# The modulation product in rows of 1024 columns, and low weight parts of three stages on VectorE

## The chip, the cores and the metric

The kernel runs on one core of a Trainium2 chip. The metric is the device time of one execution in microseconds. Before the change the median of 3 runs is 2245.02 us (2243.89 to 2248.35).

## The reference

Two transformer layers and a third, mixed one over 512 tokens of width 1024, all in float32. What matters here is the first layer and the vector that conditions it:

```python
c_act = silu(c)                                   # one row of 1024
mod = c_act @ ada_w[layer] + ada_b[layer]         # 1024 x 6144, for both layers
sh_m, sc_m, g_m, sh_f, sc_f, g_f = split(mod, 6)
h = rms_norm(x) * g * (1 + sc_m) + sh_m
u, v = split(gelu(h @ w_in + b_in), 2)            # gMLP, 2048 wide each
v = layer_norm(v); v = tril(w_s) v + b_s
x = x + g_m * rms_norm((u * v) @ w_out)
h = rms_norm(x) * g * (1 + sc_f) + sh_f
x = x + g_f * rms_norm((silu(h @ w_g) * (h @ w_u)) @ w_down)
k, v, dcum = shared_kv(x, c_act @ kv_ada_w + kv_ada_b, ...)
```

The modulation product is a row of 1024 times matrices of 6144, 2048 and 6144 columns, some 59 MB of weights, of which each element is used once.

## The kernel before

Five engines run their own instruction streams and meet at semaphores. A matrix product keeps float32 precision by splitting both operands in a high part (fp32r, rounded) and a low part (the rest): each weight times activation becomes three TensorE products, hi x hi, hi x lo and lo x hi. The work is a list of stages: mlp_u, mlp_v, mlp_out, gu0, down0, then k, v, q and so on. A stage has groups (i, j) of 256 output columns, a group has units of up to 4 chunks of 128 rows. mlp_u and mlp_v have 8 groups of 2 units, mlp_out 4 of 4, gu0 22 of 2, down0 4 of 6.

A unit's way: SP loads it into one of 4 slots of the tile `raw` (`load_unit`), once `w_used` says that TensorE has finished with the unit four before. ScalarE rounds it into `w_hi` (`split_hi`, L700). GpSimd subtracts, `w_lo = raw - w_hi`, in place of raw (`split_lo`, L706). TensorE waits for `w_split` and uses it (`gemm`, L1258). `lead` orders the splitting engines: the split of group g+1 stands before the epilogue of group g, that of group g+2 behind it. TensorE has two accumulators `acc`, so an epilogue has one group's time.

The activations go a similar way: VectorE writes tmp (`normed`), ScalarE rounds (`hi_chunks`), GpSimd subtracts (`lo_chunks`).

The modulation product is spread beside the stages as 56 steps of 256 columns. A step loads 1024 x 256 weights in two halves (`ada_load`, rows of 1 KB), VectorE multiplies each chunk of 128 rows by its column of c_act and adds (`ada_step`, L1625 and L1629, 8 instructions), and TensorE sums over the partitions with two products of one column (`ada_column`, L1309), which VectorE adds to the bias (`ada_finish`, L1634). Steps 0 to 7 belong to the setup and stay as they are. Steps 8 to 45 are one per group in mlp_u, mlp_v and gu0; TensorE's column products for a step stand at the end of the group and wait for `ada_ready`. Steps 46 to 55 are in down0. SP's order is written by hand: in these stages the weights of a group, then the step's two halves, each behind `ada_used`.

In gu0 the epilogue of a group is: ScalarE takes silu (L934), VectorE multiplies (L1816) and rounds to act_hi (L1818), GpSimd subtracts (act_lo, L1193). In mlp_v VectorE adds the bias (L1766), ScalarE takes gelu, and VectorE its statistics (L1771). mlp_u's epilogue is ScalarE's alone. The gains of an output stage are spread over the partitions by TensorE (`spread_gain`, L1316) from a diagonal that VectorE makes (`gain_diagonal`, L1672); for down0 TensorE does this at chunk 16 of the first group.

mlp_u, mlp_v and gu0 are hardware loops over i, mlp_out and down0 are unrolled.

Of the kernel before, what the change touches and what calls it, by code (L numbers as in the profile page):

```python
# [30 lines left out]
ds = bass.ds  # L31
# [26 lines left out]
ADA_STEPS = 56  # L58
DOWN_STEP, DOWN_FROM, DOWN_EVERY = 46, 24, 6
# [21 lines left out]
class Stage:  # L81


    def __init__(self, name, iters, kchunks, reader, token_major=False, second=None):
        self.name, self.iters, self.reader, self.token_major = name, iters, reader, token_major
# [9 lines left out]
    Stage("mlp_u", 4, DC, "act"), Stage("mlp_v", 4, DC, "dve", True), Stage("mlp_out", 2, GC, "dve", True),  # L95
    Stage("gu0", 11, DC, "dve"), Stage("down0", 2, FC, "dve", True),
# [10 lines left out]
def number_stages():  # L107

    unit = group = 0
    count = {"act": 0, "dve": 0}  # L110
    for s in STAGES:
        s.unit0, s.group0, s.read0 = unit, group, count[s.reader]
# [7 lines left out]
def build_program(nc, io):  # L120
    S = number_stages()
    ctx = ExitStack()
    with ctx:
# [51 lines left out]
        sq = place("sq", [P, 2, T])  # L175
        inv_diag = place("inv_diag", [P, NB, P])
# [19 lines left out]
        ada_raw = place("ada_raw", [P, 2, KU, COLS], at=ph + 88 * K)  # L196
# [86 lines left out]
        w_split = sem("w_split")  # L283
# [128 lines left out]
        def ada_round(step):  # L412

            return step - ADA_SETUP

        def ada_load(sp, w, c0, step):
            n = ada_round(step)
            for half in range(2):
                sp.wait_ge(ada_used, 2 * n + half + 1)
                sp.dma_start(ada_raw[:, half], w[half * 512:half * 512 + 512, ds(c0, COLS)].rearrange("(k p) n -> p k n", p=P)) \  # L420
                    .then_inc(ada_landed[half], 16)
# [298 lines left out]
        def _(sp):  # L720
# [36 lines left out]
            KV0, KV1 = 24, 32  # L757
            for i in range((KV1 - KV0) // 2):
                for j in range(2):
                    load_group(sp, "gu0", i, j)  # L760
                    ada_load(sp, kv_ada_w, COLS * (2 * i + j), KV0 + 2 * i + j)
            def layer1(i, j):
                ada_load(sp, ada_w[1], COLS * (KV0 - KV1 + 2 * i + j), KV0 + 2 * i + j)
            load_stage(sp, "gu0", layer1, skip=KV1 - KV0)
            st, step = S["down0"], DOWN_STEP
            for g in range(st.groups):
                for x, (k0, nk) in enumerate(st.units[g % 2]):
                    load_unit(sp, st, src_of["down0"], g // 2, g % 2, x)
# [371 lines left out]
        def _(pool):  # L1140
# [39 lines left out]
            lead(pool, "mlp_v", split_lo, nothing, None)  # L1180
# [5 lines left out]
            lead(pool, "mlp_out", split_lo, nothing, "gu0", unroll=True)  # L1186
# [8 lines left out]
            lead(pool, "gu0", split_lo, gu_epilogue, "down0")  # L1195
# [56 lines left out]
        def _(pe):  # L1252
# [8 lines left out]
            def gemm(name, hi, lo, ready, ready0, after=None, unroll=False, second=None, before_chunk=None):  # L1261
# [4 lines left out]
                def body(i):  # L1266
                    for j in range(2):
# [31 lines left out]
            def ada_column(step, par, setup=False):  # L1299

                n = step - ADA_PAIRS
                pe.wait_ge(ada_ready, n + 1)
                if not setup:
                    pe.wait_ge(ada_col, n + 1)
                column_sums(ada_ps[:, 2 * par:2 * par + 2], ada_acc[:, par, :]).then_inc(ada_sum, 1)

# [796 lines left out]
```

## Time and profile before

| | |
|---|---|
| device time, median of 3 | 2245.02 us |
| span of the profiled execution, first to last instruction | 2241.8 us |
| TensorE products busy | 2021.4 us (90%) |
| VectorE, ScalarE, GpSimd busy | 935.1, 766.3, 1009.6 us |
| mean granted TensorE clock | 0.957 |
| DMA, mean | 104 GB/s |

The page gives no time of its own execution beside the span; the median of the runs lies 3.2 us above it. TensorE's products are pipelined, so that its busy time overlaps itself and a stage is better read by its length, its count of products and its waits. Idle time of another engine says nothing unless TensorE waits for it. mlp_u runs from 53.0 to 152.4 us, mlp_v from 160.3 to 260.9, mlp_out from 285.5 to 380.8, gu0 from 401.4 to 684.2 and down0 from 684.7 to 823 us.

### The profile page before, as it was taken

Reading aid. Unit: us, or ns where it says so; the run is one execution under the profiler, and the core shown is the slowest. Engines: PE = TensorE matmul, PEld = TensorE weight load, DVE = VectorE, ACT = ScalarE, POOL = GpSimd, SP = SyncE. Lnnn points to the kernel's source line nnn. Section 1 sums busy time; section 2 is a strip of 40 time slices with the busy share of each in tenths; the row PEclk is TensorE's granted clock in tenths of the full one; section 3 lists DMA queues with packets and bytes.
Section 4 is the critical chain, followed back from the end, with each engine's and each line's share of the span. In section 5 each row is a group of like instructions: output and inputs, shape, how many; then the busy total and the mean of one; then the engine's idle time right before and its main releaser. Section 6 shows DMA issues by size and latency. Waiting matters only on the chain.

```text
span 2241.8 us, 32732 instructions
## 1 busy us (share of the span) xinstructions
PE 2021.4 (90%) x12052; PEld 1770.2 (79%) x12052; DVE 935.1 (42%) x1624; ACT 766.3 (34%) x1198; POOL 1009.6 (45%) x573
## 2 busy tenths in 40 slices
PE   5999897899999978999997999999799993987997
PEld 5789897777779976977886888899667883766897
DVE  6567742676654654544633100010337720125212
ACT  3422332432321233345644333322423320445323
POOL 2443373554454325455644555544423440625452
PEclk8999999899999989999998999999899997898999
DMA  7644323355553532222112333322212335211122
GB/s 261 196 155 151 121 68 103 108 164 164 173 171 122 190 109 59 84 76 88 52 49 61 99 94 94 102 85 91 73 57 66 94 94 85 84 38 38 48 95 85
DMA packets 274914, 232.47 MB, mean 104 GB/s; under 512 B 15017, under 2 KB 268753, under 8 KB 274561
## 3 DMA queue, kind: packets, MB, share of 16 engines
q1 hardware_dynamic: 274312, 230.97, 33.6%
q8 instruction: 68, 1.11, 0.2%
q10 hardware_dynamic: 504, 0.15, 0.0%
q14 instruction: 30, 0.24, 0.0%
HBM read 226.33 MB, written 4.75 MB: 103 GB/s over the span
## 4 chain that ended last, share of the span: by engine, by line
PE 73%; DVE 14%; DMA 3%; ACT 3%; issue 3%; DVEq 2%; SPq 1%; POOL 1%; ACTq 1%
PE acc L1258 62%; DVE ada_acc L1629 7%; PE ms L602 2%; PE acc L577 2%; DMA raw<-in_w_in 2%; DVE ada_acc L1625 1%; DVE x_tok L1707 1%; PE aux L591 1%; PE aux L1258 1%; SPq L356 1%; DMA x_tok<-in_x 1%; PE ada_ps L1309 1%; DMA ada_raw<-in_ada_w 1%; PE aux L1440 1%; DVEq L1709 1%
## 5 line engine op out<-in xcount | busy, mean ns | idle before, releaser
L706 POOL TENSOR_TENSOR w_lo<-raw,w_hi 128x1024 fp32r<-128x1024 f32 (+1 forms) x300 | 720.6, 2416 | 805.3 <-ACT w_hi L700 804.8
L1258 PE MATMUL acc<-hh,w_hi 128*128 128x512 f32 x1344 | 540.4, 402 | 45.4 <-ACT ogate L994 38.3
L1258 PE MATMUL acc<-hl,w_hi 128*128 128x512 f32 x1344 | 532.1, 396 | 0.0
L1258 PE MATMUL acc<-hh,w_lo 128*128 128x512 f32 x1344 | 532.0, 396 | 0.0
L700 ACT ACTIVATE w_hi<-raw 128x1024 fp32r<-128x1024 f32 (+1 forms) x300 | 308.6, 1040 | 505.0 <-DMA raw<-in_ffn_w_down 202.3
L1258 PEld LDWEIGHTS acc<-hh,w_hi 128*128 128x128 f32 x1344 | 258.2, 192 | 107.9 <-ACT ogate L994 38.7
L1258 PEld LDWEIGHTS acc<-hh,w_lo 128*128 128x128 f32 x1344 | 257.6, 192 | 55.5
L1258 PEld LDWEIGHTS acc<-hl,w_hi 128*128 128x128 f32 x1344 | 257.8, 192 | 54.8 <-issue 2.0
L1629 DVE SCALAR_TENSOR_TENSOR ada_acc<-ada_raw,c_act,ada_acc 128x256 f32<-128x256 f32 x336 | 265.5, 790 | 29.4 <-DMA ada_raw<-in_ada_w 3.5
L1258 PE MATMUL acc<-w_hi,hh 128*128 128x256 f32 x704 | 201.1, 286 | 0.7 <-issue 0.7
L1258 PE MATMUL acc<-w_hi,act_hi 128*128 128x256 f32 x704 | 201.6, 286 | 0.0
L1258 PE MATMUL acc<-w_hi,act_lo 128*128 128x256 f32 x704 | 199.9, 284 | 0.0
L1258 PE MATMUL acc<-w_lo,act_hi 128*128 128x256 f32 x704 | 199.9, 284 | 0.0
L1258 PE MATMUL acc<-w_lo,hh 128*128 128x256 f32 x704 | 199.2, 283 | 0.0
L1258 PE MATMUL acc<-w_hi,hl 128*128 128x256 f32 x704 | 199.2, 283 | 0.0
L1816 DVE TENSOR_TENSOR tmp<-acc,tmp 128x512 f32<-128x512 f32 x44 | 30.4, 691 | 314.4 <-ACT tmp L934 311.2
L1193 POOL TENSOR_TENSOR act_lo<-tmp,act_hi 128x512 f32 (+1 forms) x44 | 56.9, 1293 | 187.0 <-DVE act_hi L1818 187.0
L1258 PEld LDWEIGHTS acc<-w_hi,hh 128*128 128x128 f32 x704 | 135.1, 192 | 1.9 <-issue 1.4
L1258 PEld LDWEIGHTS acc<-w_hi,act_hi 128*128 128x128 f32 x704 | 135.9, 193 | 0.5 <-issue 0.5
L1258 PEld LDWEIGHTS acc<-w_lo,act_hi 128*128 128x128 f32 x704 | 135.8, 193 | 0.5 <-issue 0.5
L1258 PEld LDWEIGHTS acc<-w_hi,act_lo 128*128 128x128 f32 x704 | 135.8, 193 | 0.0
L1258 PEld LDWEIGHTS acc<-w_lo,hh 128*128 128x128 f32 x704 | 135.1, 192 | 0.8 <-issue 0.7
(367 smaller groups left out, 3086.9 us busy)
## 6 DMA issues: line engine op xcount, KB each, us to landing
raw<-in_ffn_w_gu SPq DMA_DIRECT2D x176, 256.0 KB, 3.2
ada_raw<-in_ada_w SPq DMA_DIRECT2D x80, 512.0 KB, 3.9
raw<-in_w_in SPq DMA_DIRECT2D x52, 512.0 KB, 3.4
raw<-in_ffn_w_down SPq DMA_DIRECT2D x40, 512.0 KB, 3.4
raw<-in_a_w_in SPq DMA_DIRECT2D x32, 512.0 KB, 5.0
raw<-in_a_w_out SPq DMA_DIRECT2D x16, 512.0 KB, 3.4
ada_raw<-in_kv_ada_w SPq DMA_DIRECT2D x16, 512.0 KB, 3.3
raw<-in_kv_w SPq DMA_DIRECT2D x16, 512.0 KB, 3.5
```

Source lines behind the costliest of these rows:

```text
L356: sp.dma_start(dst, ap).then_inc(landed[s], 16)
L577: pe.matmul(bank(b)[:, 0:WIDTH[b]], a["qz"][:, e, b * P:(b + 1) * P], a["k"][:, ds(i, 1), 0:WIDTH[b]].rearrange("p a t -> p (a t)"), start ...
L591: last = pe.transpose(out[:, c:c + P], a["p"][:, e, OFF[b] + s * P:OFF[b] + (s + 1) * P], ident[:])
L602: last = pe.matmul(ms[:, b * 64:b * 64 + 64], a["pT"][:, c:c + P], a["v"][:, s, ds(h * 64, 64)], start=s == 0, stop=s == b)
L700: act.activation(w_hi[:, s, 0:nk, :], raw[:, s, 0:nk, :], ACT.Copy).then_inc(w_split_hi, 1)
L706: pool.tensor_tensor(w_lo[:, s, 0:nk, :], raw[:, s, 0:nk, :], w_hi[:, s, 0:nk, :].bitcast(F32), ALU.subtract).then_inc(w_split, 1)
L1193: pool.tensor_tensor(act_lo[:, ds(f, 1), :], tmp[:, 2 + j:3 + j, :], act_hi[:, ds(f, 1), :].bitcast(F32), ALU.subtract).then_inc(act_ready, 1)
L1258: ins = pe.matmul(out, w, x, start=first and n == 0, stop=last and n == len(pairs) - 1, skip_group_check=check)
L1309: ins = pe.matmul(dst[:, m:m + 1], src[:, m * P:(m + 1) * P], ones[:, 0:1], start=True, stop=True)
L1440: pe.matmul(aux[:, t % 2, :], head_ones[:], sq[:, t % 2, :], start=True, stop=True).then_inc(hs_ps, 1)
L1629: ins = dve.scalar_tensor_tensor(total, w[:, kk, :], c_act[:, k0 + kk:k0 + kk + 1], total, ALU.mult, ALU.add)
L1816: dve.tensor_tensor(tmp[:, 2 + j, :], sums(j)[:, 1, :], tmp[:, j, :], ALU.mult).then_inc(acc_read["dve"], 1)
```

## The change

- The modulation product behind the setup is made in 12 wide steps of 1024 columns. A chunk n is one load of 128 x 1024 (rows of 4 KB) and one VectorE instruction over 1024 columns into `ada_wide`; 8 chunks make a wide step. A slot is two chunks; there are 48 slots.
- TensorE's column products are 8 per wide step (`wide_columns`), at chunk 2 of the first group of the next four (`wide_beside`), by name in mlp_out and down0. The two at every group's end go.
- Slots 0 to 7 lie in mlp_u, 8 to 15 in mlp_v, 16 to 23 behind the first two `product_group`s of mlp_out, 24 to 45 in gu0, 46 and 47 between gu0's last epilogue and down0's gain diagonal. Down0's own steps go.
- w_lo of mlp_u, mlp_v and gu0 is made on VectorE. There `lead` puts the split of the next group before the slot and the epilogue. mlp_u's first two units stand between chunks 3 and 4 of h0, gu0's first two in `add_normed` behind x_tok. `w_split` becomes one semaphore per engine.
- The three stages' loops are unrolled on the engines that the change touches (SP, TensorE, VectorE); for gu0 GpSimd's is unrolled too.

```diff
+    Stage("mlp_u", 4, DC, "act", lo="dve"), Stage("mlp_v", 4, DC, "dve", True, lo="dve"), Stage("mlp_out", 2, GC, "dve", True),
+    Stage("gu0", 11, DC, "dve", lo="dve"), Stage("down0", 2, FC, "dve", True),
...
+        def ada_load(sp, n):
+            wide, k = 2 + n // DC, n % DC
+            w, c0 = (ada_w[0], wide) if wide < 6 else (kv_ada_w, wide - 6) if wide < 8 else (ada_w[1], wide - 8)
+            sp.wait_ge(ada_used, n + 1)
+            sp.dma_start(ada_raw[:, n % 2, :], w[k * P:(k + 1) * P, ADA_WIDE * c0:ADA_WIDE * (c0 + 1)]).then_inc(ada_landed[n % 2], 16)
+        def ada_slot_load(sp, slot):
+            ada_load(sp, 2 * slot)
+            ada_load(sp, 2 * slot + 1)
...
+                eng.wait_ge(w_split_hi, unit_no(st, i, j, x) + 1)
+                eng.tensor_tensor(w_lo[:, s, 0:nk, :], raw[:, s, 0:nk, :], w_hi[:, s, 0:nk, :].bitcast(F32),
+                                  ALU.subtract).then_inc(w_split[st.lo], 1)
...
+            ada_slot_load(sp, 0)
+            ada_slot_load(sp, 1)
+            load_stage(sp, "mlp_u", lambda i, j: ada_slot_load(sp, 2 * i + j), skip=2, unroll=True)
+            load_stage(sp, "mlp_v", lambda i, j: ada_slot_load(sp, 8 + 2 * i + j), unroll=True)
+            load_group(sp, "mlp_out", 0, 0)
+            load_group(sp, "mlp_out", 0, 1)
+            st = S["mlp_out"]
             for j in range(2):
-                ada_load(sp, ada_w[0], COLS * (8 + j), 8 + j)
-            load_stage(sp, "mlp_u", lambda i, j: ada_load(sp, ada_w[0], COLS * (8 + 2 * i + j), 8 + 2 * i + j), skip=2)
-            load_stage(sp, "mlp_v", lambda i, j: ada_load(sp, ada_w[0], COLS * (16 + 2 * i + j), 16 + 2 * i + j))
-            load_stage(sp, "mlp_out")
...
+                for x in range(len(st.units[j])):
+                    ada_slot_load(sp, 16 + len(st.units[0]) * j + x)
+                    load_unit(sp, st, src_of["mlp_out"], 1, j, x)
+            load_stage(sp, "gu0", lambda i, j: ada_slot_load(sp, 24 + 2 * i + j), unroll=True)
+            load_group(sp, "down0", 0, 0)
+            ada_slot_load(sp, 46)
+            ada_slot_load(sp, 47)
+            load_stage(sp, "down0", skip=1)
...
-            split_lo(pool, S["mlp_u"], 0, 0)
             lo_chunks("h0", DC, hh, hl)
-            lead(pool, "mlp_u", split_lo, nothing, "mlp_v")
...
-            lead(pool, "mlp_v", split_lo, nothing, None)
             split_lo(pool, S["mlp_out"], 0, 0, slice(0, 1))
             for x in range(GC // KU):
                 lo_chunks("y", KU, y_hi, y_lo, KU * x)
                 split_lo(pool, S["mlp_out"], 0, 0, slice(x + 1, x + 2))
-            lead(pool, "mlp_out", split_lo, nothing, "gu0", unroll=True)
+            lead(pool, "mlp_out", split_lo, nothing, None, unroll=True)
             lo_chunks("h1", DC, hh, hl)
...
-            lead(pool, "gu0", split_lo, gu_epilogue, "down0")
+            for f in range(FC):
+                if f == FC - 1:
+                    split_lo(pool, S["down0"], 0, 0)
+                gu_epilogue(S["gu0"], f // 2, f % 2)
...
+            def wide_columns(q):
+                pe.wait_ge(ada_ready, ADA_SETUP - ADA_PAIRS + q + 1)
+                pe.wait_ge(ada_col, ADA_SETUP - ADA_PAIRS + q)
+                for m in range(ADA_WIDE // P):
+                    ins = pe.matmul(ada_ps[:, m:m + 1], ada_wide[:, m * P:(m + 1) * P], ones[:, 0:1], start=True, stop=True)
+                ins.then_inc(ada_sum, 1)
+            def wide_beside(slot0):
+                def before_chunk(i, j, k):
+                    slot = slot0 + 2 * i + j
+                    if k == 2 and slot % 4 == 0 and slot:
+                        wide_columns(slot // 4 - 1)
+                return before_chunk
...
-            gemm("mlp_u", hh, hl, h_ready, CH["h0"], lambda i, j: ada_column(8 + 2 * i + j, j))
+                ada_column(s, s % 2)
+            gemm("mlp_u", hh, hl, h_ready, CH["h0"], unroll=True, before_chunk=wide_beside(0))
...
+                if (i, j, k) in ((0, 0, 8), (1, 0, 2)):
+                    wide_columns(3 + i)
...
-                n, off = divmod((2 * i + j) * FC + k - DOWN_FROM, DOWN_EVERY)
-                if off == 0 and 0 <= n < ADA_STEPS - DOWN_STEP:
-                    ada_column(DOWN_STEP + n, n % 2)
+                if (i, j, k) == (0, 1, 2):
+                    wide_columns(ADA_WIDES - 1)
...
-            def ada_step(step, par):
-                ada_finish(step - 2, par, step - ADA_PAIRS)
-                for half in range(2):
+            def ada_chunk(n):
+                q, k = divmod(n, DC)
+                if k == 0 and q:
+                    wide_finish(q - 1)
+                dve.wait_ge(ada_landed[n % 2], 16 * (n // 2 + 1))
+                if k == 0:
+                    dve.tensor_scalar(ada_wide[:], ada_raw[:, n % 2, :], c_act[:, 0:1], None, ALU.mult).then_inc(ada_used, 1)
+                else:
                     dve.drain()
-                    dve.wait_ge(ada_landed[half], 16 * ada_round(step) + 16)
-                    ada_chunks(ada_acc[:, par, :], ada_raw[:, half], half * KU).then_inc(ada_used, 1)
-                dve.drain().then_inc(ada_ready, 1)
+                    dve.scalar_tensor_tensor(ada_wide[:], ada_raw[:, n % 2, :], c_act[:, k:k + 1], ada_wide[:], ALU.mult, ALU.add) \
+                        .then_inc(ada_used, 1)
+                if k == DC - 1:
+                    dve.drain().then_inc(ada_ready, 1)
+            def ada_slot(slot):
+                ada_chunk(2 * slot)
+                ada_chunk(2 * slot + 1)
+            def wide_finish(q):
+                dve.wait_ge(ada_sum, ADA_SETUP - ADA_PAIRS + q + 1)
+                cols = slice(2 * ADA_SETUP + DC * q, 2 * ADA_SETUP + DC * (q + 1))
+                dve.tensor_tensor(mod[:, cols], ada_ps[:, 0:DC], par_a[:, cols], ALU.add).then_inc(ada_col, 1)
...
+                    if k == 4 and between is not None:
+                        between()
...
+            def u_epilogue(st, i, j):
+                ada_slot(2 * i + j)
+            lead(dve, "mlp_u", split_lo, u_epilogue, "mlp_v", unroll=True)
...
+                if g < 2:
+                    for slot in range(16 + 4 * g, 20 + 4 * g):
+                        ada_slot(slot)
             modulation(par_b[:, 32:40], mod[:, 32:40])
-            add_normed(0, y_mlp)
+            add_normed(0, y_mlp, between=lambda: split_lo(dve, S["gu0"], 0, 0))
...
+            def gu0_epilogue(st, i, j):
+                ada_slot(24 + 2 * i + j)
+                gated(st, 0, i, j)
+            lead(dve, "gu0", split_lo, gu0_epilogue, None, unroll=True)
+            ada_slot(46)
+            ada_slot(47)
             gain_diagonal(par_b[:, 48:56], mod[:, 40:48])
             gain_copy(1)
...
+            for g in range(4):
+                product_group(1, g, y_h)
+                if g == 1:
+                    wide_finish(ADA_WIDES - 1)
```

## Rows read from the trace of the kernel before

**Rows 1.** The page's part 4, the chain that ended last, by line
```profile
PE acc L1258 62%; DVE ada_acc L1629 7%; PE ms L602 2%; PE acc L577 2%; DMA raw<-in_w_in 2%; DVE ada_acc L1625 1%; DVE x_tok L1707 1%; PE aux L591 1%; PE aux L1258 1%; SPq L356 1%; DMA x_tok<-in_x 1%; PE ada_ps L1309 1%; DMA ada_raw<-in_ada_w 1%; PE aux L1440 1%; DVEq L1709 1%
```

**Rows 2.** Windows: engine's busy us (instructions), granted clock, DMA share, GB/s
```profile
53.01:152.40 99.39, 94.74 (x412) 78.06 (x413) 54.97 (x77) 36.42 (x41) 50.30 (x24) 0.96 0.61 197
...
160.26:260.90 100.64, 97.23 (x799) 95.85 (x798) 74.92 (x114) 20.03 (x19) 30.56 (x12) 1.00 0.47 152
...
285.50:380.75 95.25, 93.60 (x779) 92.83 (x777) 27.06 (x27) 25.41 (x49) 48.37 (x25) 1.00 0.30 95
380.75:401.37 20.62, 6.90 (x34) 5.28 (x33) 15.58 (x18) 13.14 (x26) 7.85 (x4) 0.67 0.09 26
401.37:684.21 282.84, 263.10 (x1140) 213.97 (x1140) 187.32 (x244) 88.37 (x91) 146.69 (x73) 0.96 0.52 159
684.82:823.00 138.18, 135.27 (x1100) 133.49 (x1100) 65.09 (x103) 27.22 (x49) 47.04 (x22) 0.99 0.49 157
```

**Rows 3.** Waits 401.3:684.8 us: engine, line, released by: total us, times, longest
```profile
PE ada_ps L1309 <- DVEq L1620: 19.2, 12, 4.4
```

**Rows 4.** The chain of waits in order of time, 0:1100 us: start, us, what
```profile
71.79 12.46 PE acc L1258 x48
84.58 11.05 PE acc L1258 x48
95.97 11.05 PE acc L1258 x48
...
383.94 1.28 DVE x_tok L1707
```

**Rows 5.** Timeline, TensorE, 64:72 us: start, us, what, [idle before, releaser]
```profile
71.00 0.79 PE L1309 MATMUL ada_ps<-ones,ada_acc 128*128 128x1 f32 x4 [4.65 <-DVEq L1620]
```

**Rows 6.** Timeline, VectorE, 160:190 us, GpSimd idle until 175.4
```profile
161.76 1.23 DVE L1672 TENSOR_TENSOR gain_row<-ident,bcol 128x1024 f32<-128x1024 f32 x1
...
163.68 3.86 DVE L1629 SCALAR_TENSOR_TENSOR ada_acc<-ada_raw,c_act,ada_acc 128x256 f32<-128x256 f32 x7
171.93 1.22 DVE L1766 TENSOR_TENSOR v<-acc,b_in 128x1024 f32 x1 [4.39 <-PE acc L1258]
174.54 1.41 DVE L1771 BATCH_NORM_STATS2 stats<-v  x4 [1.38 <-ACT v L903]
```

**Rows 7.** Timeline, VectorE, 436:462 us
```profile
435.11 7.82 DVE L1629 SCALAR_TENSOR_TENSOR ada_acc<-ada_raw,c_act,ada_acc 128x256 f32<-128x256 f32 x7
444.76 0.69 DVE L1816 TENSOR_TENSOR tmp<-acc,tmp 128x512 f32<-128x512 f32 x1 [1.84 <-ACT tmp L934]
```

**Rows 8.** Timeline, VectorE, 40:66 us
```profile
40.89 7.69 DVE L1629 SCALAR_TENSOR_TENSOR ada_acc<-ada_next,c_act,ada_acc 128x256 f32<-128x256 f32 x7
```

**Rows 9.** Timeline, GpSimd, 44:72 us
```profile
43.20 5.09 POOL L706 TENSOR_TENSOR w_lo<-raw,w_hi 128x1024 fp32r<-128x1024 f32 x2 [39.02 <-ACT w_hi L700]
51.57 10.93 POOL L1168 TENSOR_TENSOR hl<-tmp,hh 128x512 fp32r<-128x512 f32 x8 [3.27 <-ACT hh L879]
```

**Rows 10.** The page's part 6, DMA issues: count, KB, median us to landing
```profile
raw<-in_ffn_w_gu SPq DMA_DIRECT2D x176, 256.0 KB, 3.2
ada_raw<-in_ada_w SPq DMA_DIRECT2D x80, 512.0 KB, 3.9
```

**Rows 11.** Windows of 1 us at the start, rows of 4 KB (x_tok) loading
```profile
15.00:16.00 1.00, 1.00 (x6) 1.00 (x6) 0.85 (x3) 0.00 (x0) 0.00 (x0) 1.00 1.05 418
```

**Rows 12.** Windows of 0.5 us in mlp_v, rows of 1 KB loading
```profile
187.00:187.50 0.50, 0.50 (x7) 0.50 (x6) 0.50 (x2) 0.00 (x0) 0.00 (x0) 1.00 0.99 334
```

**Rows 13.** The page's part 5: group, xcount, busy us, mean ns, idle before
```profile
L700 ACT ACTIVATE w_hi<-raw 128x1024 fp32r<-128x1024 f32 (+1 forms) x300 | 308.6, 1040 | 505.0 <-DMA raw<-in_ffn_w_down 202.3
```

**Rows 14.** Timeline, VectorE, 660:720 us
```profile
701.72 0.69 DVE L1816 TENSOR_TENSOR tmp<-acc,tmp 128x512 f32<-128x512 f32 x1 [17.61 <-ACT tmp L934]
...
703.38 2.10 DVE L1672 TENSOR_TENSOR gain_row<-ident,bcol 128x1024 f32<-128x1024 f32 x1 [0.28 <-issue]
```

**Rows 15.** Timeline, TensorE, 700:710 us
```profile
709.28 1.02 PE L1316 MATMUL acc<-gain_row,ones 128*128 128x512 f32 x2
```

More of the change, by code:

```diff
@@ L81, with __init__ @@
 class Stage:
-    def __init__(self, name, iters, kchunks, reader, token_major=False, second=None):
-        self.name, self.iters, self.reader, self.token_major = name, iters, reader, token_major
+    def __init__(self, name, iters, kchunks, reader, token_major=False, second=None, lo="pool"):
+        self.name, self.iters, self.reader, self.token_major, self.lo = name, iters, reader, token_major, lo
         def units(k):
@@ L110, in number_stages @@
     count = {"act": 0, "dve": 0}
+    split = {"pool": 0, "dve": 0}
     for s in STAGES:
-        s.unit0, s.group0, s.read0 = unit, group, count[s.reader]
+        s.unit0, s.group0, s.read0, s.split0 = unit, group, count[s.reader], split[s.lo]
+        split[s.lo] += s.per_body * s.iters
         unit += s.per_body * s.iters
@@ L175, in build_program @@
         sq = place("sq", [P, 2, T])
+        ada_wide = place("ada_wide", [P, ADA_WIDE], at=cursor[0])
         inv_diag = place("inv_diag", [P, NB, P])
@@ L1297, in gemm, with ada_column @@
                 times(pe, st.iters, body, unroll or st.per_body % RING != 0)
[L1299 to L1304, printed above, removed]
-                column_sums(ada_ps[:, 2 * par:2 * par + 2], ada_acc[:, par, :]).then_inc(ada_sum, 1)
+            def ada_column(step, par):
+                pe.wait_ge(ada_ready, step - ADA_PAIRS + 1)
+                column_sums(ada_ps[:, 2 * par:2 * par + 2], ada_acc[:, par, :]).then_inc(ada_sum, 1)
+            def wide_columns(q):
[10 more added lines that the diff above has]
+                return before_chunk
             def column_sums(dst, src):
@@ L1707, in add_normed @@
                     dve.scalar_tensor_tensor(x_tok[:, b, :], y[:, b, :], small[:, 4 + b:5 + b], x_tok[:, b, :], ALU.mult, ALU.add).then_inc(x_ready, 1)
+                if between is not None:
+                    between()
                 for half in range(2):
@@ L1736, in _ @@
             modulation(par_b[:, 0:8], mod[:, 8:16])
-            normed("h0", scol[:], mod[:, 0:8], kept=x_first, kept_sem=kept_ready)
-            def u_body(i):
-                for j in range(2):
-                    ada_step(8 + 2 * i + j, j)
-            times(dve, S["mlp_u"].iters, u_body)
+            normed("h0", scol[:], mod[:, 0:8], kept=x_first, kept_sem=kept_ready,
+                   between=lambda: split_lo(dve, S["mlp_u"], 0, 0))
+            def u_epilogue(st, i, j):
+                ada_slot(2 * i + j)
+            lead(dve, "mlp_u", split_lo, u_epilogue, "mlp_v", unroll=True)
             for q in range(4):
@@ L1758, in _, with v_epilogue @@
             dve.wait_ge(b_in_in, 16)
-            st = S["mlp_v"]
-            def v_body(i):
-                for j in range(2):
-                    ada_step(16 + 2 * i + j, j)
-                    wait_sums(dve, st, i, j)
-                    c = COLS * (2 * i + j)
-                    dve.tensor_tensor(v[:, :, ds(c, COLS)], sums_tok(j), b_in[:, ds(c, COLS)].unsqueeze(1).broadcast_to([P, NB, COLS]),
-                                      ALU.add).then_inc(acc_read["dve"], 1)
-                    dve.drain().then_inc(v_added, 1)
-                    dve.wait_ge(v_gelu, 2 * i + j + 1)
-                    for b in range(NB):
-                        dve.bn_stats(stats[:, b, ds(2 * i + j, 1), :].rearrange("p a s -> p (a s)"),
-                                     v[:, b, ds(c, COLS)])
-            times(dve, st.iters, v_body)
+            def v_epilogue(st, i, j):
+                ada_slot(8 + 2 * i + j)
+                wait_sums(dve, st, i, j)
+                c = COLS * (2 * i + j)
+                dve.tensor_tensor(v[:, :, c:c + COLS], sums_tok(j), b_in[:, c:c + COLS].unsqueeze(1).broadcast_to([P, NB, COLS]),
+                                  ALU.add).then_inc(acc_read["dve"], 1)
+                dve.drain().then_inc(v_added, 1)
+                dve.wait_ge(v_gelu, 2 * i + j + 1)
+                for b in range(NB):
+                    dve.bn_stats(stats[:, b, 2 * i + j, :], v[:, b, c:c + COLS])
+            lead(dve, "mlp_v", split_lo, v_epilogue, None, unroll=True)
             dve.drain()
@@ L1820, in _, with gated @@
-            feed_forward("gu0", 0, 24)
+            def gated(st, l, i, j):
+                wait_sums(dve, st, i, j)
+                f = 2 * i + j
+                dve.wait_ge(sg_ready, l * FC + f + 1)
+                dve.wait_ge(act_ready, l * FC + f + 1)
+                dve.tensor_tensor(tmp[:, 2 + j, :], sums(j)[:, 1, :], tmp[:, j, :], ALU.mult).then_inc(acc_read["dve"], 1)
+                dve.drain()
+                dve.tensor_copy(act_hi[:, ds(f, 1), :], tmp[:, 2 + j:3 + j, :]).then_inc(a_hi, 1)
@@ L1879, in _, with gu1_body @@
             normed("h3", scol[:], mod[:, 88:96])
-            feed_forward("gu1", 1)
+            def gu1_body(i):
+                for j in range(2):
+                    gated(S["gu1"], 1, i, j)
+            times(dve, S["gu1"].iters, gu1_body)
             gain_diagonal(par_b[:, 56:64], mod[:, 104:112])
```

71 lines of the change are left out of this document (11 added, 60 removed).

## Prediction

> **What bounds the kernel now.** I read the chain of waits first: 62% of it is the weight products of TensorE and 8% the modulation product on VectorE (its two lines) [rows 1]. The reader is to see there that a VectorE operation stands on the path of a kernel that TensorE fills. Next the windows by stage [rows 2], which give each stage a pace: mlp_u 8 groups in 99.39 us, mlp_v 8 in 100.64 us (12.6 each), gu0 22 in 282.84 us (12.86 each). The waits say what TensorE waited for in gu0: 12 times for VectorE's ada_ready before the two one-column products that end every group, 19.2 us in all [rows 3]. What a group costs without such a wait is in the chain by time: 48 products in 11.05 us, the next group 11.39 us later [rows 4], so 0.34 us for the column products and a little more in the products behind them. The group just after a wait of 4.65 us [rows 5] took 12.46 us [rows 4]: 1.4 us, in which products stand at the lower of the two clock levels (the stage's granted clock is 0.96, mlp_v's 1.00 [rows 2]). So gu0 lies 22 x (12.86 - 11.39) = 32 us over its pace, mlp_v 8 x (12.58 - 11.39) = 9.5 us.
>
> Why VectorE is late: seven steps of the sum over 256 columns take 3.86 us alone [rows 6] and 7.82 us beside GpSimd's w_lo subtractions [rows 7]; at the start 7 take 7.69 us, and the two w_lo subtractions, 5.09 us from 43.20, cover the last two [rows 8, 9]. Both engines wait for each other.
>
> The Trainium skill ("SBUF — State Buffer", "SBUF: two separate sides") says that a VectorE instruction with two SBUF inputs and a GpSimd instruction that reads SBUF take one shared port pair in turn, whole instructions at a time. The rows agree (one step 0.55 us alone, about 2.4 us behind a subtraction).
>
> **The change, part by part.** I sum against the profiled span, 2241.8 us; the median of the runs, 2245.02 us, is 3.2 us above it, and I add these back.
>
> *Cost of the new VectorE work.* A w_lo unit (1024 elements, two SBUF inputs) costs what gain_row's product costs alone, 1.23 us [rows 6]. A step of the sum over 1024 columns costs what x_tok's does before GpSimd starts, 1.28 us [rows 4]. Per group two of each, with hand-overs 5.2 us. Beside this mlp_v has the bias add 1.22, the wait for gelu 1.38 with its own lead of some 0.2, the statistics 1.41 [rows 6]: 9.6 to 9.8 us, under 10.95. gu0 has a product of 0.69 [rows 7] and a copy, at most as much: 6.6 us. As a sum VectorE is not the bound anywhere, and GpSimd, which keeps only h0, h1 and act_lo here, no longer blocks it.
>
> *What TensorE loses and gains.* The column products at each group's end go (16 + 22 groups), and with them the wait. In their place stand eight column products every fourth group, two chunks into it, for a sum that was finished one group earlier: 4 x 0.34 + about 0.15 = 1.5 us each; bounds 0.5 (it hides in the weight loads) and 2.5 us. A group without columns: 11.05 us less the slow start behind a column, 10.95 us. Average with a quarter of a wide one: 11.3 us.
>
> *The new loop.* This is the step that decides. SP issues in program order: weights of group g+1 stand behind the second ada chunk of slot g, and that waits until VectorE has consumed the chunks of slot g-1; VectorE makes w_lo of group g+1 before it starts slot g. From the end of slot g-1: issue 0.1; two fixed us of a transfer (256 KB land in 3.2 us, 512 KB in 3.9 [rows 10], less the flow); the flow of one chunk in 4 KB rows at 418 GB/s [rows 11], 1.3 us, and of 1 MB of weights in 1 KB rows at 334 GB/s [rows 12], 3.0 us; together 6.4. ScalarE's w_hi of the last unit 1.04 [rows 13] and hand-over: 1.15. w_lo 1.33. Slot g 2.65. Sum 11.5 us, equal to TensorE's 11.3 within what I know. From below: the weights land 3.4 us after an issue at 1.3 us without queueing, 9.8 us. From above: all 2 MB at 334 GB/s after the slot's end, plus 2, is 8.3 instead of 6.4, 13.4 us. I take 11.5, nearest to the median landings. VectorE may fall 2.7 us behind a group's end before a wide product waits (two chunks), some 3.5 before w_lo is late; 0.2 x 22 = 4.4 us less what it was ahead costs 1 to 2 us in gu0, nothing in mlp_v.
>
> The Trainium skill ("DMA: Bandwidth & Descriptors", "Where 436 GB/s comes from") lets loads from HBM reach no more than about 358 GB/s on one core. The x_tok row is above that; by the page's figure the chunk flows in 1.5 us, the loop is 11.7 us, gu0 3 to 4 us slower and the time about 2200 us.
>
> *Start and mlp_u.* GpSimd's first two subtractions leave VectorE's path, so the seven steps end 3.9 us sooner (3.8 instead of 7.69 [rows 8]). The two units come back in the middle of h0's eight chunks, before TensorE's first product: four chunks (4.3 us) and one unit, with a wait behind GpSimd's hl (8 take 10.93 us [rows 9]), so it starts 0.4 us sooner. The first group's wait of 4.65 us and slow 1.4 us go [rows 4, 5], 8 columns at 0.44 (11.39 - 10.95) go, 3.5 us, one wide comes (+1.5): with the start 8.5 us. VectorE then ends slot 7 after TensorE ends the stage, and the transposes' copies stand behind it: some 2.1 us lost, bounds 0 and 4. Net -6.4 us.
>
> *mlp_v*: 8 x 10.95 + 2 x 1.5 = 90.6 instead of 100.64: -10 us.
>
> *mlp_out.* Eight slots now lie behind the first two output groups on VectorE, and SP interleaves their loads with the weights of groups 2 and 3. Each slot waits for a load that waits for a ring slot, every 5.8 us (a quarter of a group: four take 95.25 us, of which the first waits some 2.5 [rows 2]); slots 16 to 19 end some 25 us after the first group, TensorE asks for them at 26. Cost: one wide product, +1.5 (the first hides in waits for y); if VectorE is late here, up to 3 more.
>
> *Into gu0* (20.62 us [rows 2]): x_tok's four steps run alone, 4 x 1.3 instead of 9.1 us (the row of 1.28 [rows 4] is one that did), but gu0's two w_lo units (2.5) follow on the same path: -1.3 us.
>
> *gu0*: 22 x 10.95 + 6 x 1.5 + 1.5 = 251.4 instead of 282.84: -31 us. TensorE's waits (19.2) are the larger part, the rest is the lower clock after each and the columns.
>
> *down0.* Ten column products (5 us) and the waits among them (about 3) go, one wide comes: -6.5. But slots 46 and 47 now stand before gain_diagonal on VectorE. Its last gated product is at 701.72, gain_row starts at 703.38 [rows 14], and TensorE needs it at 709.28 [rows 15]. Slot 46's load is there; slot 47's is issued only when 46 is consumed: four steps of 1.3 and one landing of 3.2 to 3.9 us put gain_row's end near 713. TensorE waits some 3.5 us and restarts slow, +4.5. Net -2; bounds -6.5 and +3.
>
> *Unrolled loops* in three stages: as many instructions run as before, and mlp_out and down0 are unrolled already with TensorE at 1.00 and 0.99 [rows 2]. Zero; cover gone, 2 us. Sum: -6.4 - 10 + 1.5 - 1.3 - 31 - 2 = -49: span 2193, time 2196 us.
>
> **Rivals.** (a) *The loop binds.* The same serial path at 11.8 to 12.3 us. For it: weights and ada share the queue, and ScalarE's silu or GpSimd's act_lo can stand in it. Against: in mlp_v the 16 engines run at 0.99 share while loading, so queued loads overlap [rows 12]. At 12.2: gu0 22 x 12.2 - 3 = 265 (-17.5), mlp_v -5, mlp_u -4, rest -2: 2216 us.
> (b) *The loop is far longer* and this is slower than before: the three stages have 38 groups at an average of 12.7 us; other parts give 2 us, so from about 12.75 us on nothing is won. At 13.4, where loads don't overlap with one another: 38 x 0.7 less 2: 2270 us. Against it stands the overlap named.
> (c) *VectorE is no shorter*: the slots wait for their data and not for GpSimd, in which case removing GpSimd wins little and only mlp_u's first wait with its slow start (6.05 us) and half of the columns (38 x 0.34 / 2 = 6.5 us) go: -12, 2233 us. Against: 7.82 to 3.86 [rows 6, 7].
> (d) *Everything overlaps*: a wide product costs 0.8 instead of 1.5 (9 x 0.7 = 6 us) and down0 has no wait (4.5 us): -59, 2186 us. For it: weight loads of TensorE run beside products. Against: the 0.34 us that two columns take.
>
> **Numbers.** Forecast 2196 us with its near variants (2190 to 2205) 0.52; (a) 0.27; (d) 0.10; (c) 0.06; (b) 0.05. Range 2184 to 2222. A difference of under 0.2% (4.5 us) cannot be told from none. Faster 0.94, same 0.02, slower 0.04.
>
> **What would show it.** gu0 some 251 us long, its granted clock 1.00; VectorE's w_lo at 1.23 and ada steps at 1.28 us; no wait of TensorE for ada_ready in gu0; a wait of about 3.5 us before gain_row's products in down0's first group; VectorE at work in the gap before mlp_v. I am wrong if the group pitch in gu0 is over 11.8 us, if TensorE waits for w_lo from VectorE there, or if SP's weight loads are issued over 12 us apart.

## The result and the profile after

The changed kernel is slower: 2268.53 us (median of 4 runs, 2266.61 to 2276.35) against 2244.45 us (2239.77 to 2248.35), ratio 1.0118 [1.0096, 1.014], 24 us. The profiled spans say the same, 2264.9 and 2241.8 us. The forecast was 2196 us. What happened is the mechanism of rival (b), a loop far longer than TensorE's pace, to which I had given 0.05. That its 2270 us lies so near is in part luck: it had 0.7 us more in each of the 38 groups of three stages, while gu0 shows 0.6 more, mlp_v 0.2 less, and much of the loss lies in the gap before mlp_v and in mlp_out.

The windows of the stages of the changed kernel (columns as in [rows 2]) answer to [rows 2]; they are mlp_u, mlp_v, gu0, down0:

```profile
51.45:154.60 103.15, 96.93 (x408) 78.65 (x408) 42.70 (x35) 34.90 (x40) 11.45 (x7) 0.94 0.51 169
168.90:267.07 98.17, 95.46 (x794) 94.88 (x793) 56.23 (x71) 20.01 (x19) 0.00 (x0) 1.00 0.49 154
...
412.60:708.67 296.07, 267.00 (x1157) 216.13 (x1157) 131.83 (x140) 88.48 (x92) 38.80 (x31) 0.96 0.51 151
708.67:847.60 138.93, 133.06 (x1076) 130.62 (x1076) 14.50 (x18) 27.56 (x50) 51.71 (x24) 0.98 0.31 99
```

VectorE's busy time in gu0 fell as meant, from 187.32 [rows 2] to 131.83 us, and yet gu0 takes 296.07 us for 282.84. TensorE idles 29 us in it, and its granted clock is still 0.96. Where the 24 us came in, from the starts of the stages in both traces: mlp_v starts 7.9 us later than before (a wait of 6.07 us for ws_t's copy on VectorE stands ahead of it), 1.8 come back in mlp_v, 5 go between mlp_v's end and gu0, 12.6 in gu0, 0.7 from down0 to the start of k.

The page's part 4 (the chain that ended last, by engine and by line) and three rows of its part 6 (count, KB, median us to landing), beside [rows 1, 10]:

```profile
PE 73%; DVE 9%; DMA 8%; ACT 3%; issue 2%; DVEq 1%; SPq 1%; ACTq 0%; POOL 0%
PE acc L1257 61%; DMA raw<-in_a_w_in 4%; PE ms L606 2%; DVE ada_wide L1636 2%; PE acc L581 2%; DMA raw<-in_w_in 2%; DMA raw<-in_ffn_w_gu 1%; DVE w_lo L710 1%; ACT w_hi L704 1%; PE ada_ps L1308 1%; SPq L360 1%; DVE x_tok L1738 1%; PE aux L595 1%; PE aux L1257 1%; DMA x_tok<-in_x 1%
...
raw<-in_ffn_w_gu SPq DMA_DIRECT2D x176, 256.0 KB, 3.3
ada_raw<-in_ada_w SPq DMA_DIRECT2D x80, 512.0 KB, 4.5
raw<-in_a_w_in SPq DMA_DIRECT2D x32, 512.0 KB, 7.1
```

The modulation product has shrunk in the chain (7% and 1% in [rows 1], ada_wide 2% now). In its place stand the transfers of these stages' own weights, in_a_w_in 4% and in_ffn_w_gu 1%, which [rows 1] does not have. The waits of gu0 (who waited <- for whom: us in total, times, longest) name the order of the loop:

```profile
ACT w_hi L704 <- DMA raw<-in_ffn_w_gu: 176.9, 40, 10.4
DVE w_lo L710 <- ACT w_hi L704: 141.7, 40, 7.6
...
PE acc L1257 <- issue: 23.1, 11, 3.0
...
PE ada_ps L1308 <- DVEq L1639: 4.9, 4, 1.3
```

VectorE is idle for 141.7 us waiting for w_hi, ScalarE for 176.9 us waiting for weights. TensorE waits 28.0 us: 23.1 before products (marked "issue"; each ends just as a w_lo is made) and 4.9 before wide column products, against 19.2 us in [rows 3]. The chain in order of time (start, us, what; pieces of some hundredths left out) walks round the loop in mlp_u, and then in gu0:

```profile
81.15 0.43 SPq L360
...
81.62 6.83 DMA raw<-in_a_w_in
...
88.48 1.06 ACT w_hi L704
...
89.56 1.23 DVE w_lo L710
...
90.88 1.28 DVE ada_wide L1636
...
93.57 0.34 SPq L421
...
449.99 5.72 PE acc L1257 x24
455.70 0.41 SPq L360
...
456.15 6.60 DMA raw<-in_ffn_w_gu
...
462.77 1.06 ACT w_hi L704
...
463.86 1.23 DVE w_lo L710
```

In mlp_u every piece releases the next. One turn is 12.8 us here (80.75, the end of a slot, to 93.55) and 13.2 the next time; in gu0 the slots end at 454.10, 467.84, 480.86, 494.89 and 508.89, 13.7 us a turn. Over the whole of mlp_u and gu0 the turns take 12.4 to 14.2 us. In gu0 the chain comes to the last weight load from TensorE: 7 of these loads also wait up to 0.3 us, 1.6 us in all, for the slot of raw that TensorE's late products free. SP's timeline shows the same (start, us, what):

```profile
79.38 1.72 SPq L421 DMA_DIRECT2D ada_raw<-in_ada_w  x2
81.15 0.98 SPq L360 DMA_DIRECT2D raw<-in_a_w_in  x2
92.20 1.72 SPq L421 DMA_DIRECT2D ada_raw<-in_ada_w  x2
93.96 0.98 SPq L360 DMA_DIRECT2D raw<-in_a_w_in  x2
```

(SPq is SP's queue; L421 issues ada chunks, L360 weights.) SP issues one ada chunk when VectorE has done with the first chunk of a slot, the other when it has done with the second, and only then weights. The loads run in one burst per turn. Windows of 0.5 us (the last two columns are DMA share and GB/s; the third number of busy time is VectorE's):

```profile
80.00:80.50 0.50, 0.50 (x4) 0.41 (x3) 0.50 (x1) 0.00 (x0) 0.00 (x0) 1.00 0.55 74
...
82.50:83.00 0.50, 0.50 (x3) 0.40 (x3) 0.00 (x0) 0.00 (x0) 0.00 (x0) 1.00 0.54 131
...
85.50:86.00 0.50, 0.50 (x4) 0.41 (x3) 0.00 (x0) 0.00 (x0) 0.00 (x0) 1.00 1.04 365
...
88.50:89.00 0.50, 0.00 (x0) 0.00 (x0) 0.50 (x1) 0.50 (x1) 0.00 (x0) 1.00 0.00 0
```

From 80.0 to 88.0 they carry 2.1 MB, 262 GB/s on average, with a hole at 82.5 to 83.5 (131 GB/s in the window shown) where the ada chunks run out and the weights have not begun. Then the 16 DMA engines stand still for 4.5 us while ScalarE and VectorE work. No resource of the loop is busy more than 8 of its 13 us.

### The profile page after: what moved, and what is told of

Same layout as the page of the kernel before. It is cut to its first block, busy times and chain, and to the rows that moved or that the text cites. A ratio compares the mean times of both kernels' runs of the same rounds, so it can differ in the third digit from the quotient of the medians.

```text
span 2264.9 us, 30955 instructions
## 1 busy us (share of the span) xinstructions
PE 2029.1 (90%) x12052; PEld 1773.7 (78%) x12052; DVE 819.4 (36%) x1374; ACT 765.9 (34%) x1198; POOL 822.7 (36%) x497
## 4 chain that ended last, share of the span: by engine, by line
PE 73%; DVE 9%; DMA 8%; ACT 3%; issue 2%; DVEq 1%; SPq 1%; ACTq 0%; POOL 0%
PE acc L1257 61%; DMA raw<-in_a_w_in 4%; PE ms L606 2%; DVE ada_wide L1636 2%; PE acc L581 2%; DMA raw<-in_w_in 2%; DMA raw<-in_ffn_w_gu 1%; DVE w_lo L710 1%; ACT w_hi L704 1%; PE ada_ps L1308 1%; SPq L360 1%; DVE x_tok L1738 1%; PE aux L595 1%; PE aux L1257 1%; DMA x_tok<-in_x 1%
## 5 line engine op out<-in xcount | busy, mean ns | idle before, releaser
L710 POOL TENSOR_TENSOR w_lo<-raw,w_hi 128x1024 fp32r<-128x1024 f32 (+1 forms) x224 | 531.6, 2386 | 788.7 <-ACT w_hi L704 788.4
L1189 POOL TENSOR_TENSOR act_lo<-tmp,act_hi 128x512 fp32r<-128x512 f32 (+1 forms) x44 | 56.8, 1290 | 350.0 <-DVE act_hi L1845 350.0
L710 DVE TENSOR_TENSOR w_lo<-raw,w_hi 128x1024 fp32r<-128x1024 f32 x76 | 97.9, 1294 | 223.7 <-ACT w_hi L704 222.4
L1257 PEld LDWEIGHTS acc<-w_hi,hl 128*128 128x128 f32 x704 | 135.1, 192 | 0.0
```

The source lines that it names most:

```text
L710: eng.tensor_tensor(w_lo[:, s, 0:nk, :], raw[:, s, 0:nk, :], w_hi[:, s, 0:nk, :].bitcast(F32), ALU.subtract).then_inc(w_split[st.lo], 1)
L1189: pool.tensor_tensor(act_lo[:, ds(f, 1), :], tmp[:, 2 + j:3 + j, :], act_hi[:, ds(f, 1), :].bitcast(F32), ALU.subtract).then_inc(act_ready, 1)
L1257: ins = pe.matmul(out, w, x, start=first and n == 0, stop=last and n == len(pairs) - 1, skip_group_check=check)
```

## The experiments

The theory after the result, L in the texts below: a serial loop, from here on the ring, sets the pace (SP's program order puts the weights of group g+1 behind the ada chunks of slot g, whose places are free when VectorE has used those of slot g-1; VectorE's puts slot g behind w_lo of group g+1), and cutting it at any one point gives back the forecast. Its rivals: VectorE is too slow as an engine (V); the 2 MB of a group cannot be loaded any faster (D); or the wide rows or the w_lo on VectorE cost by themselves.

**x1_sp: cut the loop at SP.** The weights of the next group now stand ahead of a slot's chunks. The lines are those of mlp_u and mlp_v; gu0 is changed in the same way:

```
-            ada_slot_load(sp, 1)
-            load_stage(sp, "mlp_u", lambda i, j: ada_slot_load(sp, 2 * i + j), skip=2, unroll=True)
+            for g in range(2, 16):
+                load_group(sp, "mlp_u" if g < 8 else "mlp_v", g % 8 // 2, g % 2)
+                ada_slot_load(sp, g - 1)
+            ada_slot_load(sp, 15)
```

> The changed kernel with one thing different: in mlp_u, mlp_v and gu0 SP issues the weights of group g+1 ahead of the two ada chunks of slot g, not behind those of slot g+... (the ada loads stand one group later in SP's order). Same loads, same instructions. Theory L (a serial loop: end of slot g-1 on VectorE, ada loads, weight loads behind them, w_hi, w_lo, slot g; about 13.2 us a group in the changed kernel's trace): the loop is cut, since weights no longer wait for VectorE. The three stages go back to TensorE's pace of 11.3 to 11.5 us a group: mlp_u -8, mlp_v -8, gu0 from 296 to 253 us, together -55 to -60: 2268 to about 2210 us. Theory D (the 2 MB a group cannot be loaded faster beside everything, rows of 4 KB load slower than thought): no change, 2268 us, DMA share near 1 for most of a group. Theory V (w_lo on VectorE makes it the bound): no change, 2268 us.

Measured 2204.77 us, ratio to the kernel before 0.9809 [0.978, 0.9837]; the profiled span is 41.7 us under that of the kernel before, where the forecast had 49. Its gu0 (window and SP's timeline):

```profile
391.00:641.25 250.25, 250.25 (x1154) 208.79 (x1153) 137.75 (x138) 87.38 (x91) 49.61 (x30) 1.00 0.58 179
...
465.26 6.36 SPq L360 DMA_DIRECT2D raw<-in_ffn_w_gu  x4
471.66 0.98 SPq L421 DMA_DIRECT2D ada_raw<-in_ada_w  x2
476.14 6.36 SPq L360 DMA_DIRECT2D raw<-in_ffn_w_gu  x4
```

Twenty-two groups in about 250.6 us with the clock at 1.00 and TensorE never idle, against 251.4 in the forecast: the same work, in another order of issue. The ada chunks now land in 6.2 us (median) for 4.5. VectorE waits for them (21.3 us in gu0), but TensorE for nothing. The same bytes flow at 179 GB/s for 151, so rival D falls too. SP's four weight loads spread over 6.4 us because they now wait for slots of raw, which TensorE frees. Against the changed kernel's 296.07 us it is 45 less, of which 28.0 were waits.

**x2_dve: cut it at VectorE.** The slot comes before the split of the next group's weights, by a helper of its own in the three stages:

```
+            for g in range(st.groups):
+                slot(slot0 + g)
+                if g + 1 < st.groups:
+                    split(eng, st, (g + 1) // 2, (g + 1) % 2)
+                elif following:
+                    split(eng, S[following], 0, 0)
+                epilogue(st, g // 2, g % 2)
```

> The changed kernel with one thing different: on VectorE, in mlp_u, mlp_v and gu0, slot g stands before the w_lo split of group g+1, not behind it. SP's order stays as changed. Theory L: the slot no longer waits for the weights that stand behind it in SP's queue; from the end of slot g-1 its chunks land in 4.5 us and take 2.65, 7 us, so the loop is far under TensorE's pace: about 2210 us as with SP's order. Theories D and V: 2268 us, as bytes and VectorE's work are the same.

Measured 2204.33 us, 0.9815 [0.979, 0.984]. SP's order is that of the changed kernel, VectorE has the same instructions; only their order differs. Two cuts at different points give the same time: it was the ring of orders, not one of its members. Both leave w_lo and the wide steps on VectorE, so rival V falls.

**x3_pool: the wide rows without the move of w_lo.** The loops of SP, TensorE and VectorE stay unrolled as in the change; w_lo of the three stages stays on GpSimd (`Stage("gu0", 11, DC, "dve")` without `lo="dve"`, `lead(pool, "gu0", split_lo, gu_epilogue, "down0")` as before).

> The wide rows of the modulation product alone: w_lo of mlp_u, mlp_v and gu0 is made on GpSimd as before the change; slots, SP's order, wide column products and unrolling are as changed. Theory L: w_lo is out of the loop (slot g waits only for its own chunks), so it is cut here too, but VectorE's steps again wait behind GpSimd's subtractions (up to 2.4 us each): 2210 to 2225 us. Theory V: the same, since VectorE is relieved of 2.5 us a group. Theory D: 2268 us. With the first two experiments this tells V from L: V wants only this one fast, L all three.

Measured 2207.32 us, 0.9821 [0.9801, 0.9842]; gu0 250.7 us. GpSimd's timeline in it:

```profile
439.99 5.72 POOL L710 TENSOR_TENSOR w_lo<-raw,w_hi 128x1024 fp32r<-128x1024 f32 x2
447.29 1.28 POOL L1192 TENSOR_TENSOR act_lo<-tmp,act_hi 128x512 f32 x1 [1.58 <-DVE act_hi L1846]
448.52 5.19 POOL L710 TENSOR_TENSOR w_lo<-raw,w_hi 128x1024 fp32r<-128x1024 f32 x2
```

Two units still take GpSimd over 5 us, as in [rows 9], but two wide steps a slot have room beside them where eight short ones had not: the slot no longer waits for weights, and TensorE waits for nothing in gu0 at 11.4 us a group. So moving w_lo, half of the change, brings nothing that can be measured (the intervals of x1_sp and x3_pool overlap), and it is what closes the ring.

**x8_lo_only: the other half alone.** The kernel before, w_lo of the three stages on VectorE (whose loops there are unrolled), the old steps of 256 columns.

> The other part alone: the kernel before with w_lo of mlp_u, mlp_v and gu0 on VectorE ahead of each step (the order of the change), and the old steps of 256 columns with two column products at each group's end. Theory L: the loop exists here too, and is longer, since a step takes 4.3 us alone: end of step, half load and weights 6.5 to 7, w_hi 1.1, w_lo 1.3, step 4.8: 13.7 to 14.2 us against 12.7 before: slower than before, 2285 to 2305 us. If only the removed blocking of GpSimd counted (3.9 us less of VectorE's time a group, 2.5 more), it would be faster than before: some 2225 us.

Measured 2300.77 us, 1.0242 [1.021, 1.0273]. Its chain in gu0 is the same ring with a longer slot (L1631 are the steps over 256 columns, seven of them behind one another):

```profile
442.69 0.51 SPq L358
...
446.04 4.57 DMA raw<-in_ffn_w_gu
...
450.63 1.07 ACT w_hi L702
...
451.73 1.23 DVE w_lo L708
...
453.54 0.48 DVE ada_acc L1631
```

This turn takes 15.2 us (442.28 to 457.43). Alone, w_lo's move costs 2.4%; the wide rows with unrolled loops bring 1.8%, of which unrolling by itself may be up to 0.6 (x6_unroll below); the wide rows in the old loops were not run. Here the steps do run at 0.48 us and not at 1.1 [rows 7], so the port is free, and it is no use: the ring sets the time.

**x9_half: fewer bytes in the landing.** Each ada chunk loads 512 of its 1024 columns, and these are read twice; the kernel leaves out half of the modulation weights, and its rows of a chunk are 2 KB and not 4.

```
-            sp.dma_start(ada_raw[:, n % 2, :], w[k * P:(k + 1) * P, ADA_WIDE * c0:ADA_WIDE * (c0 + 1)])...
+            sp.dma_start(ada_raw[:, n % 2, 0:ADA_WIDE // 2], w[k * P:(k + 1) * P, ADA_WIDE * c0:ADA_WIDE * c0 + ADA_WIDE // 2])...
```

> The changed kernel, with each ada chunk loading only its first 512 columns, which VectorE reads twice (half of the modulation weights behind the setup are left out, so these columns of the modulation are wrong). Every instruction, wait and order is the same, VectorE's instructions are as long. It measures the disputed term, the time from the end of a slot to the landing of the next weights (7.6 to 8.6 us in the changed kernel, 6.4 in the forecast). If it is the flow of bytes at some 260 to 300 GB/s, each group saves 0.9 to 1.8 us of the loop of 13.2: 38 groups x 1.3 = 50 us at most until TensorE's pace binds: 2215 to 2235 us. If it is fixed latencies and issues, the time stays at 2268 us.

Measured 2210.55 us, 0.9841 [0.981, 0.9871], a little under the range expected. The chain in mlp_u:

```profile
78.45 0.34 SPq L421
...
79.31 5.51 DMA raw<-in_a_w_in
...
84.85 1.07 ACT w_hi L704
...
89.95 0.34 SPq L421
```

From the slot's end (78.44) to the last weights is 6.4 us, and the turn 11.5: the two figures of my prediction, reached only with 1.5 MB instead of 2 MB in a turn. Over mlp_u's turns the time to the last weights is 6.4 to 7.2 us, 6.6 on average, where the changed kernel has 7.7 to 8.6, 8.2 on average; in gu0 the averages are 7.0 and 8.65. So 0.5 MB less is worth some 1.6 us of the ring. It still sets gu0's pace: 261.2 us, 11.9 a group, against x1_sp's 11.4.

**x5_diag: the gain diagonal first.** gain_diagonal stands before slots 46 and 47.

> The changed kernel with one thing different: after gu0 VectorE makes the gain diagonal before slots 46 and 47, not behind them. The trace of the changed kernel has TensorE idle for 5.82 us in down0 before the products that spread the gain. Expected by every theory of the stages before: that wait and the slow start behind it go, -6 to -7.5 us, 2262 us; nothing else moves. If the slots then delay the copy of the gains, TensorE waits at the second group of down0 and the gain is smaller.

Measured 2263.77 us, 1.0074 [1.0051, 1.0096]: 4.8 us under the changed kernel by the medians, 10 by the ratios, each to the runs of the kernel before that were taken beside it, and the wait before gain_row's products in down0 is gone. The intervals of the two touch, so the size rests on the traces: down0's weight products span 130.7 us there and 138.9 in the changed kernel, 8.2 less (x1_sp 139.3, x7_best 130.4). The changed kernel's chain there:

```profile
730.12 4.52 DMA ada_raw<-in_ada_w
...
734.72 1.28 DVE ada_wide L1636
...
736.38 1.24 DVE gain_row L1703
...
737.76 3.75 PE acc L1328 x4
```

**x6_unroll: the kernel before, three stages unrolled.** `unroll=True` on SP, TensorE, VectorE and GpSimd (gu0), nothing else.

> The kernel before with the loops of mlp_u, mlp_v and gu0 unrolled on the engines where the change unrolls them, nothing else. Expected: no difference, 2245 +- 5 us. If unrolled code is fetched late, some us slower, and a part of the change's loss is that.

Measured 2233.08 us, 0.9943 [0.9924, 0.9963]: some 11 to 13 us, where I had put zero. To find the engine, two more:

**x11_pe_unroll: TensorE's loops alone.**

> The kernel before with TensorE's loops of mlp_u, mlp_v and gu0 alone unrolled; SP, VectorE and GpSimd keep theirs. Theory V (the 11 us of x6_unroll come from VectorE: its operations behind each turn of a loop show a wait for issue, 0.2 us some 22 times each on three lines in gu0, and VectorE is the engine that TensorE waits for): nothing here, 2241 to 2248 us. Theory T (TensorE's own loop costs at each turn): 2233 to 2236 us.

Measured 2238.78 us, 0.9977 [0.9965, 0.9989].

**x12_rest_unroll: the others alone.**

> The kernel before with the loops of SP, VectorE and GpSimd of the three stages unrolled and TensorE's kept. Theory V: as x6_unroll, 2233 to 2236 us. Theory T: 2241 to 2248 us.

Measured 2241.48 us, 0.9984 [0.9971, 0.9998]. Neither theory holds: each part brings about a third, 5 and 4 us by the ratios, and together they bring 13 [8, 17]. The intervals are too wide to say that the whole is more than its parts. VectorE's waits for issue in gu0, 11.2 us in the kernel before (us in total, times, longest), do go, to 2.7 us in x12_rest_unroll. These are the lines of the kernel before:

```profile
DVE ada_acc L1625 <- issue: 4.1, 22, 0.2
DVE act_hi L1818 <- issue: 3.8, 21, 0.2
DVE tmp L1816 <- issue: 3.3, 9, 0.4
```

But TensorE's waits for the sum in gu0 stay (19.2, 19.0, and 18.0 us in x6_unroll). Where the gain comes from is open.

**x7_best and x10_best2: a version without the loop and without the small waits.** x7_best is x1_sp with the diagonal first, the second wide product of mlp_out at chunk 5 instead of 2, and mlp_out's slots loaded one unit earlier:

```
-                if (i, j, k) in ((0, 0, 8), (1, 0, 2)):
+                if (i, j, k) in ((0, 0, 8), (1, 0, 5)):
...
+            ada_slot_load(sp, 16)
             load_group(sp, "mlp_out", 0, 1)
```

> A version meant to beat both: the changed kernel with SP's order of the first experiment, the gain diagonal ahead of slots 46 and 47, slot 16's load one group earlier and slots 17 to 23 one unit earlier in mlp_out, and mlp_out's second wide product at chunk 5, not 2. Against the first experiment (2205 us) TensorE's wait of 6.13 us in down0 goes with its slow start, -6.5, and the wait of 2.70 us in mlp_out, -3: 2195 us.

Measured 2193.78 us, 0.9772 [0.9742, 0.9803]. The earlier slots made a new wait of TensorE in mlp_out:

```profile
PE acc L1265 <- issue: 5.9, 2, 5.4
PE acc L1265 <- POOL w_lo L710: 0.7, 1, 0.7
```

x10_best2 takes that part back.

> x7_best without its change to SP's order in mlp_out: SP's lead in the three stages, the gain diagonal before slots 46 and 47, and the second wide product of mlp_out at chunk 5 instead of 2. Theory Q (in x7 the wait of 5.4 us at 350.4 came from the slot loads that were moved ahead of the weights of group (1,1)): that wait and the 0.7 us behind it go, the wait of 2.7 us for the wide product stays away: 5 to 6 us less than x7, 2187 to 2190 us. Rival (the wait comes from VectorE or the ring and not from SP's order): it stands here too, 2193 us.

Measured 2186.64 us, 0.9743 [0.9729, 0.9758], the fastest of the study. In the same stretch of mlp_out TensorE's waits are

```profile
PE acc L1262 <- issue: 0.5, 1, 0.5
```

and from mlp_v's end to gu0 it takes 140.3 us, where x1_sp, with its wait of 2.70 us for the wide product, takes 145.5.

## Why the prediction was wrong

The step that failed is *The new loop*. I had found the ring, named it the step that decides, and worked it out as 11.5 us; it is 12.4 to 14.2, on average 13.2 in mlp_u and 13.6 in gu0. From about 12.75 us, I had written, nothing is won. Term by term:

- Slot's end to weights landed: forecast 6.4 us, measured 7.7 (80.75 to 88.45), 8.1 and, in gu0, 8.65 (454.10 to 462.75). I let one chunk and the weights flow after the slot's end, 1.5 MB, as if the other chunk had by then landed. But the first chunk is issued only one wide step (1.4 us) before the slot's end and the second at it, and some 0.1 MB had flowed by then: 2.0 MB were left. The 0.5 MB that I had left out are 1.6 us at my 334 GB/s, which makes 8.0, and x9_half, with 1.5 MB, shows the 6.4 us. My upper bound of 8.3 (all 2 MB) was the true description (gu0's 8.65 lies even above it), and I had set it aside because loads overlapped in a trace whose chunks were issued well ahead. What the hole of 1 us costs by itself is not shown. Why gu0, with four loads of 256 KB, takes 0.5 to 1 us more than mlp_u with two of 512 was not tried; SP is 2.1 to 2.4 us over the issue of the four and 0.98 over that of the two, which would be enough.
- w_hi 1.11 us (1.15), w_lo with its hand-over 1.32 (1.33), slot 2.68 (2.65): right.
- *gu0*: its pace without a wait was right to 1 us (x1_sp, x3_pool, x10_best2: 250.6 to 250.7 for 251.4); the 31 us were there and were not collected.

The error of judgement: 11.5 against TensorE's 11.3 left no margin on a path whose bounds I had put at 9.8 and 13.4. The chance of the rivals (a) and (b) should have been spread evenly over that range: with 12.75 as the turning point, a fifth of it lies on the slow side.

*Start and mlp_u*: TensorE starts 1.6 us sooner (51.45), as part of the gain, but the ring binds from the third group on, and the stretch from mlp_u's last weight product to mlp_v's first grew from 7 to 14.5 us, since VectorE came 6.07 us late to the copies, and not 2.1. With the ring cut it is 6.7 us. *mlp_out* with the way into gu0: +5, where I had +1.5 - 1.3 and up to 3 more; the wide product waited 2.3 us for its sum and then took 3.58 us instead of 1.84. *down0*: the mechanism was right, the wait 5.8 us instead of 3.5. Slot 46's first step took 2.36 us and not 1.3, beside GpSimd's act_lo, and slot 47's landing 4.5 and not 3.2 to 3.9.

*mlp_v*: -1.8 instead of -10, and here a second term was wrong beside the ring. In x1_sp the stage has neither a wait nor a lower clock and still takes 96.3 us (its window, columns as in [rows 2]); x2_dve, x3_pool and x10_best2 have the same 96.3:

```profile
148.85:245.12 96.27, 96.27 (x802) 95.83 (x800) 57.12 (x76) 19.46 (x19) 0.00 (x0) 1.00 0.48 159
```

I had 90.6 from 10.95 us a group, a pace read from groups of 48 products of 512 columns. mlp_v's groups have 96 products of 256 columns, 0.12 us each, 11.5 us a group, and each of its two wide products takes 1.8 us. The ring adds only 3 us: the changed kernel loaded weights ahead in the gap before the stage.

With the ring cut, the other errors can be read by themselves. From the starts of the stages in x1_sp and the kernel before: up to mlp_v -10.8 us (forecast -6.4), mlp_v -4.9 (-10), the way into gu0 +5.0 (+0.2), gu0 -32.8 (-31), down0 with what follows it up to k +0.9 (-2). So the forecast would have been some 7 us too low even then. VectorE's 9.6 to 9.8 us a group in mlp_v add up to 9.4 from the terms given; nothing hung on it. *Unrolled loops*: zero was wrong by some 11 us in the faster direction.

*Both engines wait for each other* holds [rows 6, 7], and wide rows are enough against it with w_lo left on GpSimd (x3_pool, TensorE without a wait in gu0). The Trainium skill ("SBUF — State Buffer", "SBUF: two separate sides") describes this shared port; x8_lo_only agrees (0.48 us a step once GpSimd is away) and shows that a free port is not yet a shorter path.

Of the signs I named, all three that would prove me wrong appeared: a pitch over 11.8 us (13.5), TensorE waiting for w_lo, weight loads over 12 us apart (81.15 to 93.96).

## What to carry to other kernels

Draw the ring of program orders before moving work between engines: if engine A's next instruction waits for B, B's for a load, and the load's issue for A, its turn is the sum of all of them, whatever the engines' loads, and only overlap that a trace of that very ring shows may be taken off. Issue loads that the bound engine needs ahead of loads that follow another engine's progress, and let an engine do the step that frees a queue before the step that waits for it; either cuts the ring at no cost. Try the parts of a change singly: here one half, with the unrolled loops, was worth 1.8% and the other cost 2.4%. Read the pace of each stage from a row of that stage: products of another size ran at another pace.

## What the runs showed that I had not expected

- A load queued behind others landed far later than its median alone: the 512 KB weight loads in 7.1 us (5.0 before, 3.7 in x1_sp, where they go first).
- With nothing but loops unrolled the kernel before gains 0.57% [0.37, 0.76], and the two halves of that 0.23% and 0.16%, with intervals of 0.11 to 0.35 and 0.02 to 0.29.
- A wait costs more than itself: some 17 of gu0's 45 us between the changed kernel and x1_sp lie outside the waits, at a granted clock of 0.96 against 1.00.
- 96 products of 256 columns take 11.5 us at a granted clock of 1.00, and 48 of 512 columns 10.9 (x1_sp, mlp_v and gu0).
